# Two transformer blocks on one core: strips spread, low activations last in two tiles, feed-forward remainders on VectorE, no filler products

## The chip, the core and the metric

The kernel runs on one NeuronCore of one Trainium2 chip. The core has TensorE (PE), VectorE (DVE), ScalarE (ACT), GpSimd (POOL) and a queue for transfers (SP). The number that counts is the device time of one execution in microseconds, lower being better; the profiled execution has a time of its own beside it.

## What is computed

The reference runs 256 tokens of width 1024 through two models one behind the other, all in fp32. Each part of it has this shape (the reference, cut):

```python
h = modulate(x, norm_g[l, 0], sh1, sc1)      # rmsnorm(x) * (1 + scale) + shift
y = mixer(h)                                 # gla, or sliding window attention (swa)
x = x + g1[:, None, :] * y
h = modulate(x, norm_g[l, 1], sh2, sc2)
y = peer(h, ...)                             # product-key retrieval, u and v tables
x = x + g2[:, None, :] * y
```

The second model has the mixers mLSTM (`ml`) and latent attention (`mla`), each with a norm behind its output product, and a feed-forward part (`relu(h @ w1)` squared, `@ w2`, inner width 4096) where the first has `peer`. The vectors sh, sc and g come from `silu(c) @ mod_w + mod_b`: each is one "strip" of 8 tiles of 128x1024.

## The kernel before

**Products in three passes.** An fp32 product is made of three products of fp32r values: weight-high by activation-high, weight-high by activation-low, weight-low by activation-high. The weights stream from memory through `ring` (two slabs of two 128x1024 tiles, issued by SP). For each tile ACT makes `split_hi` (L1443), and DVE (`less_splits_vector`, L1468) or POOL (`splits_gpsimd`, L810, and `split_lo_gpsimd`, L1456) makes the remainder `split_lo = ring - split_hi`. Both are double-buffered; `hi_made`, `lo_made` count what is made, `hi_free`, `lo_free` what PE has let go. PE reads them in L698 (mixer products), L1353/L1401/L1405 and L1788 (peer), L2452/L2476/L2480 (first feed-forward product, `ffn1`) and L2494 (second, `ffn2`).

**Output products of the mixers** (`gla_out`, `swa_out`, `ml_out`, `mla_out`: `tile_gemm_M` with `last_by_tile`). PE turns the attended values (L594), ACT makes their high part (`gla_y`, `swa_y`, `ml_y`, `mla_y`, L765), DVE their low part `yT_lo` (`turned_lo_vector`, L772), and then PE takes eight weight tiles, 12 products of 128x512 each (L698). `row_store` (L486) copies a row of gains out of two banks of the accumulator memory that the product later writes. Behind the product DVE multiplies and adds the residual (L874, L885; L887 where a norm comes in between), ACT takes sums of squares (L824), DVE norms (L934, L938), and PE turns the normed tiles (L965, `tile_turn_tensor`) for the next product, the first of which are L1353 or L2452.

**Side strips.** The later modulation vectors are computed beside the mixers. POOL issues the loads (L426, `small<-in_mod`) into four slots; load n waits until DVE has used chunk n-4. DVE adds each chunk to the strip (L437 for its first chunk, L440 for the others, `side_chunks_vector`), at the places of DVE's program where the code calls it; when a strip is full PE sums it over partitions (L359, 32 products of one column), and DVE stores it (L456).

**Fillers.** `keep_busy_tensor` (L953) issues products of `ident` with `ident` into a bank that nobody reads, in nine places, 120 in all: ahead of seven turns L965, and at `swa.q` and `mla.qa` ahead of turns L579:

```python
KEEP_BUSY = {"n2_0": 8, "n1_1": 16, "n2_1": 9, "m1": 32, "m2_0": 12, "m1_1": 7, "m2_1": 9,
             "swa.q": 11, "mla.qa": 16}
```

The trace has two records for each.

**Feed-forward.** `ffn1` has 32 weight tiles of 24 products of 128x256, `ffn2` 32 tiles of 12 products of 128x512. ACT drains each pair of tiles of `ffn1` into one of four buffers (L2562, L2578); DVE squares it (L2622), rounds it to `hid_hi` (L2624) and takes `hid_lo` (L2626). POOL makes the remainders of tiles 2 to 31 of `ffn1` of both layers, tiles 0 to 3 of `ffn2` in layer 0 and all 32 in layer 1; DVE makes the other 28 of layer 0 (L1468), with the strip chunks of stage `f2_0` in between.

## Time and profile before

| | |
|---|---|
| time of three executions | 2770.6, 2771.14 and 2772.21 us (median 2771.14) |
| the profiled execution's own time | 2766.39 us |
| its span, from the first instruction to the last | 2764.8 us |
| PE busy | 2624.3 us (95%) |
| DVE busy | 2089.8 us (76%) |
| ACT busy | 1145.6 us (41%) |
| POOL busy | 714.3 us (26%) |
| data moved | 536.93 MB, 194 GB/s |

The span is what the trace's positions refer to: 1186.00 is a place 1186 us behind its start. The profiled execution took 1.6 us more than its span, and the median of the unprofiled ones lies 4.8 us above it. Busy time of PE counts matmuls, at whatever clock was granted.

### The profile page before, as it was taken

To read this page: it belongs to the slowest core of one execution; us is meant where nothing else is said; L and a number is where in the kernel's file an instruction comes from. 1 tells how busy PE (TensorE), PEld (TensorE's weight loads), DVE (VectorE), ACT (ScalarE), POOL (GpSimd) and SP (SyncE) were. 2 spreads that over 40 slices of the span, in tenths; PEclk is the share of its full clock that TensorE was granted. 3 is DMA by queue.
4 is the path that set the end of the run, shared out by engine and by line. 5 is a ranking of instruction groups with operands and counts; after the bars stand their busy time and mean duration, and the time that the engine had idled before them with its cause. 6 is when DMAs were issued, how large, how long until landed. Compare 5 with 4: busy or idle time off the path is not lost.

```text
span 2764.8 us, 51194 instructions
## 1 busy us (share of the span) xinstructions
PE 2624.3 (95%) x18482; PEld 2311.9 (84%) x18482; DVE 2089.8 (76%) x3398; ACT 1145.6 (41%) x1662; POOL 714.3 (26%) x461
## 2 busy tenths in 40 slices
PE   5989999999999999899999999999999899987998
PEld 4469999999877887789999998778888798866986
DVE  7545997777899778767987778997777798646890
ACT  1235444434434445434443334434445453322443
POOL 2001994000000000006980000000001085010787
PEclk9989999999999999999999999999999999998999
DMA  9634555444466876254555444667876446762454
GB/s 350 223 101 151 175 183 176 160 162 162 168 215 231 283 254 237 103 183 157 180 176 167 160 159 168 201 223 256 284 260 252 144 160 234 245 243 107 147 179 147
DMA packets 147627, 536.93 MB, mean 194 GB/s; under 512 B 16784, under 2 KB 17168, under 8 KB 147232
## 3 DMA queue, kind: packets, MB, share of 16 engines
q1 hardware_dynamic: 115088, 417.08, 44.7%
q0 software_dynamic: 31104, 113.26, 11.6%
q10 hardware_dynamic: 1296, 4.72, 0.4%
q8 instruction: 89, 1.46, 0.2%
q14 instruction: 50, 0.41, 0.0%
HBM read 531.85 MB, written 3.15 MB: 194 GB/s over the span
## 4 chain that ended last, share of the span: by engine, by line
PE 75%; DVE 11%; issue 6%; POOL 4%; DMA 2%; ACT 2%; DVEq 1%; SPq 0%; POOLq 0%; ACTq 0%
PE ps L1788 19%; PE ps L1401 15%; PE ps L1405 8%; PE ps L698 6%; PE ps L2494 5%; PE ps L1353 4%; POOL split_lo L1456 4%; PE ps L657 3%; PE ps L2476 3%; PE ps L1746 3%; PE ps L359 2%; DVE split_lo L1468 1%; PE ps L2480 1%; PE ps L635 1%; DMA ring<-in_stream 1%
## 5 line engine op out<-in xcount | busy, mean ns | idle before, releaser
L1443 ACT ACTIVATE split_hi<-ring 128x1024 fp32r<-128x1024 f32 x740 | 779.8, 1055 | 789.1 <-PE ps L1405 444.5
L1468 DVE TENSOR_TENSOR split_lo<-ring,split_hi 128x1024 fp32r<-128x1024 f32 x516 | 629.3, 1220 | 221.4 <-ACT split_hi L1443 221.1
L1456 POOL TENSOR_TENSOR split_lo<-ring,split_hi 128x1024 fp32r<-128x1024 f32 x208 | 551.5, 2669 | 172.1 <-ACT split_hi L1443 171.1
L376 POOL DMA_DIRECT2D mod_w<-in_mod x96 | 51.0, 531 | 1145.8 <-ACT gate L1498 426.5
L1401 PE MATMUL ps<-hT_hi,split_hi 128*128 128x256 f32 x2048 | 292.4, 285 | 0.0
L1405 PE MATMUL ps<-hT_hi,split_lo 128*128 128x256 f32 x2048 | 288.6, 284 | 2.5 <-POOL split_lo L1456 2.4
L1440 ACT ACTIVATE gate_hi<-gate 128x256 fp32r x256 | 106.9, 417 | 440.0 <-PE ps L1788 439.8
L1401 PE MATMUL ps<-hT_lo,split_hi 128*128 128x256 f32 x2048 | 287.4, 283 | 0.0
L1788 PE MATMUL ps<-split_hi,gate_hi 128*128 128x512 f32 x1024 | 284.1, 398 | 0.0
L1788 PE MATMUL ps<-split_hi,gate_lo 128*128 128x512 f32 x1024 | 276.3, 390 | 1.0 <-DVE gate_lo L1466 1.0
L1788 PE MATMUL ps<-split_lo,gate_hi 128*128 128x512 f32 x1024 | 276.6, 391 | 0.0
L1405 PEld LDWEIGHTS ps<-hT_hi,split_lo 128*128 128x128 f32 x2048 | 263.8, 192 | 5.4 <-POOL split_lo L1456 5.4
L1401 PEld LDWEIGHTS ps<-hT_lo,split_hi 128*128 128x128 f32 x2048 | 264.1, 192 | 0.0
L1401 PEld LDWEIGHTS ps<-hT_hi,split_hi 128*128 128x128 f32 x2048 | 263.0, 191 | 0.0
L1788 PEld LDWEIGHTS ps<-split_hi,gate_lo 128*128 128x128 f32 x1024 | 191.6, 188 | 43.8 <-DVE gate_lo L1466 3.0
L1788 PEld LDWEIGHTS ps<-split_lo,gate_hi 128*128 128x128 f32 x1024 | 191.4, 188 | 43.8 <-DVE split_lo L1468 3.3
L1788 PEld LDWEIGHTS ps<-split_hi,gate_hi 128*128 128x128 f32 x1024 | 187.0, 188 | 36.5 <-issue 1.4
L1466 DVE TENSOR_TENSOR gate_lo<-gate,gate_hi 128x256 fp32r<-128x256 f32 x256 | 108.0, 422 | 127.7 <-ACT split_hi L1443 127.4
L426 POOL DMA_DIRECT2D small<-in_mod x80 | 42.6, 533 | 458.1 <-DVE gate L440 319.0
L1665 DVE TENSOR_TENSOR small<-small 128x512 bf16<-128x512 bf16 x384 | 139.2, 417 | 0.0
L1746 PEld LDWEIGHTS ps<-small 128*128 128x128 bf16 x3072 | 96.8, 98 | 36.5 <-DVE small L1665 24.8
L1746 PE MATMUL ps<-small 128*128 128x64 bf16 x3072 | 111.8, 193 | 13.0 <-DVE small L1665 13.0
(383 smaller groups left out, 3886.0 us busy)
## 6 DMA issues: line engine op xcount, KB each, us to landing
ring<-in_stream SPq DMA_DIRECT2D x782, 512.0 KB, 4.1
mod_w<-in_mod POOLq DMA_DIRECT2D x96, 512.0 KB, 4.7
small<-in_mod POOLq DMA_DIRECT2D x80, 512.0 KB, 6.0
gate<-in_mod POOLq DMA_DIRECT2D x32, 512.0 KB, 9.2
gate<-in_mod ACTq DMA_DIRECT2D x8, 512.0 KB, 11.3
gate<-in_mod SPq DMA_DIRECT2D x8, 512.0 KB, 10.1
x_kept<-x POOLq DMA_DIRECT2D x4, 512.0 KB, 2.9
gate<-x_kept POOLq DMA_DIRECT2D x4, 512.0 KB, 9.1
```

The lines of the kernel that those rows point to most:

```text
L698: return nc.tensor.matmul(ps[:, banks[2 * nb + i], :], src[:, b * per + n, i * P:(i + 1) * P], w[:, b % 2, at_:at_ + BANK], start=(b == n ...
L1353: ins = nc.tensor.matmul(out, w[:, b % 2, c * P:(c + 1) * P], src[:, c, :], start=(c == 0 and w is split_hi and src is hi), stop=(c == DC ...
L1401: nc.tensor.matmul(out, split_hi[:, e, c * P:(c + 1) * P], part[:, c, :], start=(part is hT_hi and c == 0), stop=False)
L1405: ins = nc.tensor.matmul(out, split_lo[:, e, c * P:(c + 1) * P], hT_hi[:, c, :], start=False, stop=(c == DC - 1))
L1443: nc.scalar.activation(split_hi[:, e, :], ring[:, slot, e * D:(e + 1) * D], ACT.Copy).then_inc(hi_made, 1)
L1456: nc.gpsimd.tensor_tensor(split_lo[:, e, :], ring[:, slot, e * D:(e + 1) * D], split_hi[:, e, :].bitcast(F32), ALU.subtract).then_inc(lo_m ...
L1466: nc.vector.tensor_tensor(gate_lo[:, e, :], at(gate, i, 16 * SEQ, (2 * j + e) * SEQ, SEQ), gate_hi[:, e, :].bitcast(F32), ALU.subtract).th ...
L1468: nc.vector.tensor_tensor(split_lo[:, e, :], ring[:, (START[name] + j) % RING, e * D:(e + 1) * D], split_hi[:, e, :].bitcast(F32), ALU.sub ...
L1665: ins = nc.vector.tensor_tensor(pairs(hot_r[r][m]), equal, of_token(2 + m, HALF), ALU.mult)
L1746: ins = nc.tensor.matmul(ps[:, 5 + r % 2, n * HALF:(n + 1) * HALF], hot_c[r % 2][:, n, :], hot_r[r % 2][m][:, n, :], start=(m == 0), stop= ...
L1788: return nc.tensor.matmul(ps[:, 2 * nb + n, :], g[:, e, n * P:(n + 1) * P], w[:, e, nb * BANK:(nb + 1) * BANK], start=False, stop=True, sk ...
L2494: return nc.tensor.matmul(ps[:, 4 + 2 * nb + n, :], h[:, c0, n * P:(n + 1) * P], w[:, e, nb * BANK:(nb + 1) * BANK], start=(first and h is ...
```

## The change

It has seven parts. (a) In the four output products the first two weight tiles are taken by kind: weight-high and weight-low by activation-high for both tiles, and then weight-high by activation-low for both. (b) `row_store` stands ahead of `turned_lo_vector` in all four mixers. (c) The product `swa_q` writes banks 6 and 7 in place of 0 and 1. (d) All fillers are gone. (e) The strip chunks of `swa` and `mla` stand earlier in DVE's program, and none stands with the last two remainders of the output product; chunk 18 of `ml` stands earlier. (f) In `ml` the gates and the gated norms of both token tiles stand behind both attended tiles. (g) All remainders of the feed-forward parts are DVE's, between its squares; POOL issues loads only.

```diff
+            if last_by_tile:
+                for kind in (((split_hi, hi), (split_lo, hi)), ((split_hi, lo),)):
+                    for b in range(2):
+                        for w, src in kind:
+                            ready(b, w, src)
+                            for nb in range(nbs):
+                                for i in range(NT):
+                                    ins = product(b, w, src, 0, nb, i)
+                            if w is split_lo:
+                                ins.then_inc(lo_free, 1)
+                            elif src is lo:
+                                ins.then_inc(hi_free, 1)
...
+            row_store(v, "g1_0", 0)
             turned_lo_vector(v, "gla.on", yT_lo, gla_y, bank=4)
-            row_store(v, "g1_0", 0)
...
-        Q_BANKS = (2, 3, 0, 1)
+        Q_BANKS = (2, 3, 6, 7)
...
+            row_store(v, "g1_1", 4)
             turned_lo_vector(v, "swa_o", yT_lo, swa_y)
-            row_store(v, "g1_1", 4)
-            for n in range(6, 16):
-                if n < 12:
-                    less_splits_vector(v, "swa_out", n - 4, n - 3)
-                side_chunks_vector(v, "swa", n, n + 1)
+            side_chunks_vector(v, "swa", 10, 12)
+            for n in range(12, 18):
+                less_splits_vector(v, "swa_out", n - 10, n - 9)
+                if n < 16:
+                    side_chunks_vector(v, "swa", n, n + 1)
...
-            attended_vector(v, mls, ml_h, 0, [lambda: side_chunks_vector(v, "ml", 18, 19), lambda: head_gains(0)])
+            attended_vector(v, mls, ml_h, 0, [lambda: None, lambda: None])
             probT_vector(v, mls, 1)
-            heads_var_vector(v, "ml.r2", 0)
             shares(1)
-            heads_gated_vector(v, "ml.r2", 0, ml_h, ml_o, "ml.gated")
-            attended_vector(v, mls, ml_h, 1, [lambda: less_splits_vector(v, "ml_out", 0, 1), lambda: head_gains(1)])
-            heads_var_vector(v, "ml.r2", 1)
-            heads_gated_vector(v, "ml.r2", 1, ml_h, ml_o, "ml.gated")
+            attended_vector(v, mls, ml_h, 1, [lambda: head_gains(0), lambda: head_gains(1)])
+            for i in range(NT):
+                heads_var_vector(v, "ml.r2", i)
+                heads_gated_vector(v, "ml.r2", i, ml_h, ml_o, "ml.gated")
+            less_splits_vector(v, "ml_out", 0, 1)
...
+            def less(i, j, e):
+                tile = TILE0[f"ffn1_{l}"] + 2 * j + e
+                v.eng.wait_ge(hi_made, i * 8 + (tile + 1))
+                v.eng.wait_ge(lo_free, i * 8 + (tile + 1))
+                nc.vector.tensor_tensor(split_lo[:, e, :], ring[:, (START[f"ffn1_{l}"] + j) % RING, e * D:(e + 1) * D],
+                                        split_hi[:, e, :].bitcast(F32), ALU.subtract).then_inc(lo_made, 1)
+            for j in range(1, 4):
+                less(0, j, 0)
+                less(0, j, 1)
+                squares(0, j - 1)
...
+            side_chunks_vector(v, "mla", 18, 20)
+            for n in range(20, 26):
+                less_splits_vector(v, "mla_out", n - 18, n - 17)
+                if n < 24:
+                    side_chunks_vector(v, "mla", n, n + 1)
+            v.wait_ge(vector_steps, v.n)
+            tile_post_vector(v, "mla_out", "m2_1", 0)
...
             for l in range(2):
-                if l:
-                    side_loads_gpsimd(g, "mla")
-                splits_gpsimd(g, f"ffn1_{l}", 2, 8)
-                split_lo_gpsimd(g, f"ffn1_{l}", 1, 4)
-                if l:
-                    split_lo_gpsimd(g, "ffn2_1", 0, 4)
-                else:
-                    splits_gpsimd(g, "ffn2_0", 0, FFN2_FIRST)
-                    side_loads_gpsimd(g, "f2_0")
+                side_loads_gpsimd(g, ("f2_0", "mla")[l])
```

`squares(i, j)` holds the three instructions of L2622 to L2626. The functions' lines move: L486 keeps its number, L772 becomes L784, L1468 becomes L1459, L874 becomes L876, L2622 to L2626 become L2616 to L2620, and the loop's remainders are L2626.

PE's program at the start of `gla_out`, as a difference (- before, + changed), where `gla_y` is the high part of the activations and `yT_lo` the low part:

```order
 L594 MATMUL ps<-ident,gate 128x128 x16
 L698 MATMUL ps<-split_hi,gla_y 128x512 x4
-L698 MATMUL ps<-split_hi,yT_lo 128x512 x4
 L698 MATMUL ps<-split_lo,gla_y 128x512 x4
 L698 MATMUL ps<-split_hi,gla_y 128x512 x4
-L698 MATMUL ps<-split_hi,yT_lo 128x512 x4
 L698 MATMUL ps<-split_lo,gla_y 128x512 x4
+L698 MATMUL ps<-split_hi,yT_lo 128x512 x8
 L698 MATMUL ps<-split_hi,gla_y 128x512 x4
```

The two groups of products with `yT_lo` have moved from behind 4 and 16 products to behind 16, as one group of 8. It is the same in the other three output products.

DVE's program at the end of `mla_out`, before (from the last but two remainder on; L1468 is a remainder, L440 a strip chunk, L874 the first step behind the product):

```order
L1468 TENSOR_TENSOR split_lo<-ring,split_hi 128x1024
L440 SCALAR_TENSOR_TENSOR gate<-small,c_act,gate 128x1024
L1468 TENSOR_TENSOR split_lo<-ring,split_hi 128x1024
L440 SCALAR_TENSOR_TENSOR gate<-small,c_act,gate 128x1024
L1468 TENSOR_TENSOR split_lo<-ring,split_hi 128x1024
L440 SCALAR_TENSOR_TENSOR gate<-small,c_act,gate 128x1024 x4
L486 COPY gate<-ps 128x512 x2
L874 TENSOR_TENSOR gate<-ps,gate 128x512 x2
```

And the same place in the changed kernel (L1459 is the remainder, L876 the first step behind the product):

```order
L1459 TENSOR_TENSOR split_lo<-ring,split_hi 128x1024
L440 SCALAR_TENSOR_TENSOR gate<-small,c_act,gate 128x1024
L1459 TENSOR_TENSOR split_lo<-ring,split_hi 128x1024
L440 SCALAR_TENSOR_TENSOR gate<-small,c_act,gate 128x1024
L1459 TENSOR_TENSOR split_lo<-ring,split_hi 128x1024 x2
L876 TENSOR_TENSOR gate<-ps,gate 128x512 x2
L857 TENSOR_SCALAR stat<-stat 128x1
```

The four chunks at the end and the copy of the gain row L486 have moved ahead of the product, and two remainders stand together at the end.

DVE's program at the start of the loop of `ffn1_0`, before (`gate` is the drained buffer; ISA and REGISTER_ALU rows carry waits and addresses):

```order
L2622 TENSOR_TENSOR gate<-gate 128x512
L2623 ISA
L2624 ISA
L2624 COPY hid_hi<-gate 128x512
L2625 REGISTER_ALU
L2626 REGISTER_ALU
L2626 TENSOR_TENSOR hid_lo<-gate,hid_hi 128x512
```

And its first rows in the changed kernel, where L2626 is now the remainder and L2616 the square:

```order
L2626 TENSOR_TENSOR split_lo<-ring,split_hi 128x1024 x2
L2616 TENSOR_TENSOR gate<-gate 128x512
L2618 CAST hid_hi<-gate 128x512
L2620 TENSOR_TENSOR hid_lo<-gate,hid_hi 128x512
L2626 TENSOR_TENSOR split_lo<-ring,split_hi 128x1024 x2
```

Two remainders now stand ahead of each square. POOL's program over the same stretch and up to the start of layer 1, before (it makes the remainders of L810 and L1456 and issues the strip loads L426):

```order
L810 TENSOR_TENSOR split_lo<-ring,split_hi 128x1024 x4
L426 DMA small<-in_mod 128x1024 x40
L810 TENSOR_TENSOR split_lo<-ring,split_hi 128x1024 x6
L1449 UNCONDITIONAL_BRANCH
L1449 ISA
L1456 TENSOR_TENSOR split_lo<-ring,split_hi 128x1024
```

And the end of POOL's program in the changed kernel:

```order
L376 DMA mod_w<-in_mod 128x1024
L383 REGISTER_ALU
L383 COMPARE_AND_BRANCH
L2867 DMA gate<-x_kept 128x1024 x2
L426 DMA small<-in_mod 128x1024 x64
L131 UNCONDITIONAL_BRANCH
```

The 64 loads of both layers now stand in one row behind each other, each held only by its slot; no remainder is left on POOL.

## Rows read from the trace of the kernel before

**Rows 1.** The page: busy time, costliest groups (busy, mean ns), DMA issues (to landing).

```profile
PE 2624.3 (95%) x18482; PEld 2311.9 (84%) x18482; DVE 2089.8 (76%) x3398; ACT 1145.6 (41%) x1662; POOL 714.3 (26%) x461
...
L1456 POOL TENSOR_TENSOR split_lo<-ring,split_hi 128x1024 fp32r<-128x1024 f32 x208 | 551.5, 2669 | 172.1 <-ACT split_hi L1443 171.1
...
small<-in_mod POOLq DMA_DIRECT2D x80, 512.0 KB, 6.0
```

**Rows 2.** Waits of PE (engine, line, releaser: us in total, times, longest).

```profile
PE ps L359 <- DVE gate L874: 10.9, 2, 5.9
```

**Rows 3.** Timeline, start of `gla_out` (start, us, instruction, xcount, [idle before, releaser]).

```profile
174.60 2.48 DVE L772 TENSOR_TENSOR yT_lo<-ps,gla_y 128x512 fp32r<-128x512 f32 x4 [1.16 <-ACT gla_y L765]
177.00 1.28 DVE L486 COPY gate<-ps 128x512 f32<-128x512 f32 x2
...
178.38 2.04 PE L698 MATMUL ps<-split_hi,gla_y 128*128 128x512 f32 x4 [3.79 <-DVE gate L486]
```

**Rows 4.** Windows, the same place (stretch, length, busy per engine, granted clock PEclk).

```profile
176.00:183.00 7.00, 4.62 (x12) 3.66 (x13) 2.27 (x4) 0.38 (x2) 0.00 (x0) 0.52 0.00 0
```

**Rows 5.** Timeline, start of `swa_q`.

```profile
1090.25 1.69 PE L698 MATMUL ps<-split_hi,own_hi 128*128 128x512 f32 x4 [2.00 <-ACT gate L1871]
1091.20 0.87 DVE L789 SCALAR_TENSOR_TENSOR hT<-ps,scale_c,own_hi 128x256 f32<-128x256 f32 x2
```

**Rows 6.** Timeline, from the last product of `swa_out` to the next product.

```profile
1186.00 0.40 PE L698 MATMUL ps<-split_lo,swa_y 128*128 128x512 f32 x1
...
1189.33 1.29 DVE L440 SCALAR_TENSOR_TENSOR gate<-small,c_act,gate 128x1024 f32<-128x1024 f32 x1 [1.22 <-DMA small<-in_mod]
...
1191.40 6.99 PE L359 MATMUL ps<-ones,gate 128*128 128x1 f32 x32 [5.00 <-DVE gate L874]
...
1198.25 4.19 PE L953 MATMUL ps<-ident 128*128 128x128 f32 x18
...
1204.85 3.49 PE L1353 MATMUL ps<-hT_hi,split_hi 128*128 128x256 f32 x8 [0.17 <-ACT hT_hi L981]
```

**Rows 7.** Timeline, behind the last product of `gla_out`.

```profile
202.60 1.95 PE L953 MATMUL ps<-ident 128*128 128x128 f32 x16
...
209.55 3.48 PE L1353 MATMUL ps<-hT_hi,split_hi 128*128 128x256 f32 x8 [0.86 <-ACT hT_hi L981]
```

**Rows 8.** Timeline, start of `ml_out`.

```profile
2182.66 2.05 PE L698 MATMUL ps<-split_hi,ml_y 128*128 128x512 f32 x4 [2.95 <-DVE yT_lo L772]
```

**Rows 9.** Timeline, end of `mla_out`.

```profile
2548.12 0.40 PE L698 MATMUL ps<-split_lo,mla_y 128*128 128x512 f32 x1
2551.18 1.28 DVE L440 SCALAR_TENSOR_TENSOR gate<-small,c_act,gate 128x1024 f32<-128x1024 f32 x1 [2.58 <-DMA small<-in_mod]
```

**Rows 10.** Timeline of PE, first product behind `mla_out`.

```profile
2567.32 0.36 PE L2452 MATMUL ps<-mlp_hi,split_hi 128*128 128x256 f32 x1 [0.15 <-ACT mlp_hi L981]
```

**Rows 11.** Timeline, end of `ml_out` (L359 stands right behind its last product).

```profile
2206.81 3.69 PE L359 MATMUL ps<-ones,gate 128*128 128x1 f32 x32
...
2217.11 0.35 PE L2452 MATMUL ps<-mlp_hi,split_hi 128*128 128x256 f32 x1 [0.51 <-ACT mlp_hi L981]
```

**Rows 12.** Timeline, from `ffn1_0` to `ffn2_0`.

```profile
2320.08 2.92 DVE L2622 TENSOR_TENSOR gate<-gate 128x512 f32<-128x512 f32 x1
...
2324.30 0.68 DVE L2622 TENSOR_TENSOR gate<-gate 128x512 f32<-128x512 f32 x1
...
2329.54 1.95 PE L2494 MATMUL ps<-split_lo,hid_hi 128*128 128x512 f32 x4 [3.80 <-DVE split_lo L1468]
2330.07 1.22 DVE L1468 TENSOR_TENSOR split_lo<-ring,split_hi 128x1024 fp32r<-128x1024 f32 x1
```

**Rows 13.** Windows, `ffn1_0` with its first `ffn2` tiles, and `ffn2_1`.

```profile
2245.00:2329.00 84.00, 79.58 (x614) 75.86 (x612) 80.44 (x42) 35.45 (x40) 73.28 (x31) 1.00 0.57 189
...
2662.00:2753.00 91.00, 89.68 (x379) 70.98 (x380) 31.75 (x15) 33.91 (x35) 81.12 (x32) 1.00 0.51 165
```

**Rows 14.** Timeline, the 32 fillers of `m1`.

```profile
2062.52 7.31 PE L953 MATMUL ps<-ident 128*128 128x128 f32 x64
```

More of the change, by code:

```diff
@@ L713, in ready @@
                     t.wait_ge(*when((lo_mark if src is lo else hi_mark)(b * per + n)))
-            for b in range(tiles - (2 if last_by_tile else 0)):
+            if last_by_tile:
[10 more added lines that the diff above has]
+                                ins.then_inc(hi_free, 1)
+            for b in range(2 if last_by_tile else 0, tiles - (2 if last_by_tile else 0)):
                 for w, src in kinds:
@@ L801, in less_splits_vector @@
                 split_lo_vector(v, name, 0, b // 2, b % 2)
-        def splits_gpsimd(g, name, first, last):
-            g.eng.wait_ge(lo_made, TILE0[name] + first)
-            for b in range(first, last):
-                tile = TILE0[name] + b
-                g.eng.wait_ge(hi_made, tile + 1)
-                g.eng.wait_ge(lo_free, tile + 1)
-                nc.gpsimd.tensor_tensor(split_lo[:, b % 2, :], ring[:, (START[name] + b // 2) % RING, (b % 2) * D:(b % 2 + 1) * D],
-                                        split_hi[:, b % 2, :].bitcast(F32), ALU.subtract).then_inc(lo_made, 1)
         def half(nb):
@@ L943, in scale_vector @@
                                            op0=ALU.add, op1=ALU.mult).then_inc(vector_steps, v.step(f"{name}.scale"))
-        KEEP_BUSY = {"n2_0": 8, "n1_1": 16, "n2_1": 9, "m1": 32, "m2_0": 12, "m1_1": 7, "m2_1": 9,
-                     "swa.q": 11, "mla.qa": 16}
-        def keep_busy_tensor(t, place, bank):
-            for mark in free[bank]:
-                t.wait_ge(*when(mark))
-            for _ in range(KEEP_BUSY[place]):
-                nc.tensor.matmul(ps[:, bank, 0:P], ident[:, :], ident[:, :], start=True, stop=True)
         def tile_turn_tensor(t, name, bank, read_by):
-            keep_busy_tensor(t, name, bank)
             for i in range(NT):
@@ L2127, in swa_vector @@
                 less_splits_vector(v, "swa_q", b, b + 1)
+            side_chunks_vector(v, "swa", 0, 2)
             for i in range(NT):
@@ L2421, in mlstm_vector @@
                     side_chunks_vector(v, "ml", n, n + 1)
-            post_rest_vector(v, "ml_out", 4, 0, "m2_0")
+            v.wait_ge(vector_steps, v.n)
+            tile_post_vector(v, "ml_out", "m2_0", 0)
         MLP = Area(gate, LAYER)
@@ L2428, in build, with ffn2_less_vector @@
         MLP_STEPS = FF // P // 8
-        FFN2_FIRST = 4
-        def ffn2_less_vector(v):
-            v.eng.wait_ge(lo_made, TILE0["ffn2_0"] + FFN2_FIRST)
-            for b in range(FFN2_FIRST, FF // P):
-                less_splits_vector(v, "ffn2_0", b, b + 1)
-                n = b - FFN2_FIRST
-                if n % 4 < 3 and n - n // 4 < DC * len(SIDE_STRIPS["f2_0"]):
+        def ffn2_less_vector(v, l, first, last):
+            for b in range(first, last):
+                less_splits_vector(v, f"ffn2_{l}", b, b + 1)
+                n = b - 4
+                if l == 0 and n >= 0 and n % 4 < 3 and n - n // 4 < DC * len(SIDE_STRIPS["f2_0"]):
                     side_chunks_vector(v, "f2_0", n - n // 4, n - n // 4 + 1)
@@ L2627, in mlp_vector @@
+            with v.eng.Fori(1, MLP_STEPS) as i:
+                for j in range(4):
+                    less(i, j, 0)
+                    less(i, j, 1)
+                    if j:
+                        squares(i, j - 1)
+                    else:
+                        squares(i - 1, 3)
             v.seen.clear()
-            if l == 0:
-                ffn2_less_vector(v)
+            ffn2_less_vector(v, l, 0, 2)
+            squares(MLP_STEPS - 1, 3)
+            ffn2_less_vector(v, l, 2, FF // P)
@@ L2730, in mla_vector @@
                     .then_inc(vector_steps, v.step())
-            side_chunks_vector(v, "mla", 10, 14)
+            side_chunks_vector(v, "mla", 6, 12)
             for i in range(NT):
```

43 lines of the change are left out of this document (21 added, 22 removed).

## The prediction

> **What bounds the kernel now.** I read the page first. PE is busy for 2624.3 of 2764.8 us [rows 1], so PE's program sets the time, and a change can only give what lies in the remaining 140 us, or in stretches in which PE runs at the lower of its two clocks. POOL makes 208 remainders at a mean of 2.67 us each, and a strip load takes 6.0 us from issue to landing [rows 1]. Second, the waits of PE, to see which engine ends them. The largest that the change touches is that of the strip sums L359 on DVE, 10.9 us in two places [rows 2]. Third, the timeline around each of these waits, where the reader is to see what DVE did just before it let PE go. Fourth, the granted clock of the same stretches: behind the wait of 3.79 us ahead of `gla_out` it is 0.52 over 7 us [rows 4], that is 1.2 GHz. So a wait of PE costs twice: itself, and the slower products behind it.
>
> Unit prices. In `ffn2_1` 379 records of products of 128x512 filled 89.68 us [rows 13], 0.237 us each; a weight tile of 12 such products is 2.8 us, and so is one of `ffn1`, 24 products of half the width. A pair of tiles is 5.7 us. A filler record at full clock takes 7.31 / 64 = 0.114 us [rows 14].
>
> **Gains.** *Start of `gla_out`.* DVE made `yT_lo` from 174.60 on, then copied the gain row (two copies, from 177.00, 1.28 us together), and only then could PE begin, at 178.38 [rows 3]. DVE had been idle for 1.16 us ahead of 174.60 [rows 3], so the row copy, moved in front, ends near 174.8, and PE begins there: 3.6 us earlier. `yT_lo` then ends at 174.8 + 2.5 = 177.3, and its first product stands 16 products later, not before 174.8 + 16 x 0.237 = 178.6. Some of the half clock goes with the wait; the first four products took 2.04 us [rows 3] for 4 x 0.237 = 0.95. I take 1 us. Sum **4.5**, between 3.6 and 5.9 (3.6 and the 4.6 us behind 178.38 in [rows 4] at full clock, 2.3).
>
> *The other three starts.* There the turned values stand in the banks that the product writes, so PE still waits until DVE has read them for `yT_lo`; parts (a) and (b) bring nothing. In `ml` part (f) lets DVE come to `yT_lo` earlier, since the step ahead of it loses a chunk (1.29 us [rows 6]). PE began at 2182.66 after 2.95 us of waiting for it [rows 8]; I take **1.5**, between 0 and 2.95.
>
> *End of `swa_out`.* The last product starts at 1186.00, so the gemm ends near 1186.2. DVE is still adding chunks until 1189.33 + 1.29, partly waiting for the loads; PE's L359 starts at 1191.40 after 5.00 us idle, its 32 products take 6.99 us at half clock, the 9 fillers 4.19 (0.233 per record, twice 0.114), and the next product starts at 1204.85 [rows 6, 14]. That is 18.6 us. Behind `gla_out`, the same code without chunks, it is 209.55 - 202.60 = 6.95 us [rows 7]. With the chunks ahead, `swa_out` should look like that; I take 0.5 us off for the strip's sum and store: **11.2**, between 5.0 (the wait alone) and 11.7.
>
> *End of `mla_out`.* 2548.35 to 2567.32, 19.0 us [rows 9, 10], with DVE held by a chunk whose load landed 2.58 us late [rows 9]. Behind `ml_out`, whose chunks end in time, it is 2206.81 to 2217.11, 10.3 us [rows 11]. Difference 8.7, and 0.5 as in the next item: **9.2**, between 5.9 (the wait in [rows 2]) and 9.5.
>
> *Fillers that held PE.* At `m2_0` and `m1_1` fillers ran at half clock and ended behind the normed tile. By 0.233 per record, 12 and 7 of them are up to 5.6 and 3.3 us long; I estimate **1.5** for both, 0 to 3.
>
> *Feed-forward, layer 0.* While POOL makes remainders, a square takes 2.92 us, and 0.68 once it has stopped [rows 12]. DVE is therefore late: it comes to the `ffn2` remainder after its last squares, PE waits 3.80 us for it, and the next four products take 1.95 us, half clock [rows 12]. In the window PE lacks 84.0 - 79.6 = 4.4 us [rows 13]. With remainders on DVE, a pair costs it 2 x 1.22 + 3 x 0.68 = 4.5 us [rows 12] of the 5.7 that PE takes, if no POOL instruction competes. I count 4.4, and 1.7 for two groups of four products at half clock: **6.1**, between 3.8 and 8. *Layer 1* had no such wait; 91.0 - 89.7 = **1.3** [rows 13], 0 to 3.
>
> A page speaks to this step. The Trainium skill, "SBUF — State Buffer", section "Who interferes with whom", says that a VectorE instruction with two SBUF inputs and a GpSimd instruction that reads SBUF exclude each other for their whole length. The square has both inputs in SBUF, and 2.92 against 0.68 us agrees [rows 12]. By the same section the strip loads, which GpSimd issues, can be held by VectorE copies and casts; no run here shows by how much, and that rule stands beside rival C.
>
> Gains: 4.5 + 1.5 + 11.2 + 9.2 + 1.5 + 6.1 + 1.3 = **35.3 us**.
>
> **Losses.** *Fillers that covered a real wait.* At `n2_0`, `n1_1`, `swa.q`, `m1` and `mla.qa` the fillers (8, 16, 11, 32, 16) ran for 1.9, 3.7, 2.5, 7.3 and 3.7 us at 0.114 per record [rows 7, 14] while PE had to wait for the norm or the rotation anyway. Without them PE is idle for that long and a little more. The nearest row is `gla_out`: 3.79 us of idling, then half clock over 7 us [rows 3, 4], 4.6 of them with products, which costs 2.3 us; with work throughout it would be 3.5. Below, 0: another wait of the same length, 2.95 us ahead of `ml_out`, was already paid. Much of the half clock can also fall on turns that wait for ACT. I take 1.0, 1.7, 1.2, 1.2 and 1.7: **6.8**, between 0 and 17.5. At `n2_1` and `m2_1` there was no full clock to lose.
>
> *`swa_q` in banks 6 and 7.* These banks hold the turned values that DVE reads in its last L789, at 1091.20 + 0.87 = 1092.07; PE began at 1090.25 [rows 5]. PE now waits 1.85 us more, with about 1 us of clock behind it: **2.9**, between 0 (if the first banks give it enough) and 4.
>
> *High parts late.* `hi_free` for the first tile comes after 20 products, not after 9. 20 x 0.237 + 1.1 for ACT is 5.8 us, and the third tile is due at 24 x 0.237 = 5.7; with the two signals 0.4 us late: **1.6** over four products, 0 to 3.
>
> *Chunks ahead of the rotations.* They are 1.29 us each [rows 6] in places where DVE mostly waits; **0.8** in all, 0 to 4. What is queued behind them is the rotation, and PE's turns wait for it.
>
> Losses 6.8 + 2.9 + 1.6 + 0.8 = **12.1 us**. The row copies, the move of the gates in `ml` and POOL's loads cost nothing, since DVE was idle or POOL, with nothing but loads left in its queue, had only its slots to wait for; if the cover were gone, a row copy would cost 1.28.
>
> **Sum.** -35.3 + 12.1 = -23.2. The profiled execution would go from 2766.4 to 2743, the median from 2771.1 to **2748 us** (0.8%).
>
> **Rivals.** *A, the sum as above*: 0.66, 2738 to 2756.
> *B, the clock takes more.* PE falls back to 1.2 GHz at each of the five covered waits for 7 us, 3.5 each, 17.5 in place of 6.8: -12.5, 2759. For it: [rows 4]. Against: part of that time PE waits in any case. 0.15. The Trainium skill, "TensorE: Matmul & The Clock Gate", section "HAM oscillation — how this bites in real kernels", says that idle gaps of PE put it back to the low clock and that the work behind pays; by it this case would be B.
> *C, strips still late.* Loads take 6.0 us with four slots, so a chunk can come every 1.5 us, and DVE's queue has remainders of the output product behind each. If a load is late the remainder is late, and PE waits inside the gemm in place of its end. Half of 20.4 is given back: -13, 2758. For it: DVE waits for loads in both ends [rows 6, 9]. Against: the chunks start earlier by several tiles. 0.08.
> *D, slower: DVE becomes the bound of the feed-forward.* The remainder waits behind the square in DVE's order, and the square behind ACT's drain. If a pair takes DVE 7.0 us in place of 4.5, 32 pairs lose 1.3 each, 42 us, and the 7.4 gained are gone: +26, 2797. It outweighs the rest from about 6.4 us per pair. Against: 1.2 us of room per pair. 0.04.
> *E, the feed-forward change does nothing*, because the squares stay at 2.9 us for another reason or the seam wait stays: -16, 2755. 0.07.
>
> **Range and chances.** A, C and E lie at 2738 to 2758 and B around 2759, so 2737 to 2761 leaves out D and the tails of A and B. A measurement of this kernel tells about 0.2% (5.5 us) from no change. Faster: A, C, E nearly whole and most of B, 0.91; same, mostly from B with more losses, 0.05; slower, D, 0.04.
>
> **What would show it.** Squares of about 0.7 us throughout; no wait on DVE at the start of `ffn2_0`; no POOL remainder; `gla_out` at about 175; L359 right behind the last product of `swa_out` and `mla_out`, and 7 and 10 us to the next product; `swa_q` waiting for DVE L801; half-clock stretches where the five fillers were. The prediction is wrong if L359 still waits, if PE waits for L2626 in the feed-forward, or if half-clock stretches of 7 us follow at more than two of the five places where fillers covered a wait.

## The result, and the profile after

The changed kernel takes 2749.27 us (median of 4 executions, 2745.64 to 2754.17) where the kernel before takes 2771.68: ratio 0.9915, interval 0.9892 to 0.9938. Measured again beside the last experiments it took 2749.86 us (6 executions) against 2772.42, ratio 0.9923 (0.9906 to 0.994). It is 0.8% faster. The forecast was 2748 us, in 2737 to 2761.

The profiled execution took 2747.67 us, 18.7 less than that of before; the forecast for it was 2743. The page of the changed kernel, its span, busy times and the two groups of remainders (busy us, mean ns, idle before and releaser):

```profile
span 2746.0 us, 50625 instructions
...
PE 2599.7 (95%) x18242; PEld 2288.9 (83%) x18242; DVE 2049.4 (75%) x3494; ACT 1144.9 (42%) x1662; POOL 459.1 (17%) x365
...
L1459 DVE TENSOR_TENSOR split_lo<-ring,split_hi 128x1024 fp32r<-128x1024 f32 x552 | 673.1, 1220 | 273.4 <-ACT split_hi L1434 273.1
L1447 POOL TENSOR_TENSOR split_lo<-ring,split_hi 128x1024 fp32r<-128x1024 f32 x128 | 341.1, 2681 | 148.9 <-ACT split_hi L1434 148.6
```

PE is busy for 24.6 us less than before [rows 1], with 240 records fewer, which are the fillers'; so PE's busy time says nothing of the gain. POOL makes 128 remainders where it made 208 [rows 1]. DVE makes the others, in this group and in the new line L2626.

The waits of PE that the change touched (engine, line, releaser: us in total, times, longest):

```profile
PE ps L956 <- DVE stat L857: 18.7, 5, 8.0
...
PE ps L698 <- DVE yT_lo L784: 11.0, 3, 5.3
PE ps L657 <- DMA ring<-in_stream: 8.5, 2, 5.1
...
PE ps L579 <- DVE gate L2733: 4.5, 1, 4.5
PE ps L698 <- DVE hT_lo L807: 4.2, 1, 4.2
```

L359 on L874, first in [rows 2], no longer stands there. In its place stand waits that fillers had covered (L956 is the turn of a normed tile, L579 on L2733 the one at `mla.qa`), and the new one of `swa_q` on L807.

The two ends of output products, in the timeline of the changed kernel, `swa_out` first. The rows are the strip's sum, the turns and the next product:

```profile
1189.68 3.84 PE L359 MATMUL ps<-ones,gate 128*128 128x1 f32 x32
...
1193.38 3.38 PE L956 MATMUL ps<-ident,gate 128*128 128x128 f32 x16
...
1196.62 3.66 PE L1344 MATMUL ps<-hT_hi,split_hi 128*128 128x256 f32 x8
```

```profile
2541.89 4.33 PE L359 MATMUL ps<-ones,gate 128*128 128x1 f32 x32
...
2548.19 3.53 PE L956 MATMUL ps<-ident,gate 128*128 128x128 f32 x16 [1.97 <-DVE stat L857]
...
2552.18 0.35 PE L2446 MATMUL ps<-mlp_hi,split_hi 128*128 128x256 f32 x1 [0.46 <-ACT mlp_hi L972]
```

L359 stands right behind the product now, at full clock (3.84 us for 32, 6.99 in [rows 6]). From the last product of `swa_out` (1189.44) to the next product it is 7.2 us where it was 18.9, and behind `mla_out` (2541.66) 10.5 where it was 19.2 [rows 6, 9, 10]. Both are what the ends of `gla_out` and `ml_out` show [rows 7, 11].

DVE in `ffn1_0` of the changed kernel, groups by line (busy us, mean ns, idle before, releaser). L2626 is the remainder, L2616 the square, L2618 the high part, L2620 the low part:

```profile
L2626 DVE TENSOR_TENSOR split_lo<-ring,split_hi 128x1024 fp32r<-128x1024 f32 x22 | 26.9, 1223 | 14.2 <-ACT split_hi L1434 14.2
L2620 DVE TENSOR_TENSOR hid_lo<-gate,hid_hi 128x512 f32 x12 | 8.3, 693 | 1.5
L2616 DVE TENSOR_TENSOR gate<-gate 128x512 f32<-128x512 f32 x11 | 7.5, 684 | 0.0
L2618 DVE CAST hid_hi<-gate 128x512 f32 x11 | 4.7, 427 | 1.6 <-DVE gate L2616 0.3
```

Every square takes 0.68 us, where [rows 12] has 2.92. Windows over the two feed-forward products of layer 0 (length, busy of PE, PEld, DVE, ACT, POOL, granted clock, DMA share, GB/s):

```profile
2241.00:2305.00 64.00, 64.00 (x546) 64.00 (x545) 46.74 (x57) 28.97 (x34) 0.00 (x0) 1.00 0.58 188
2307.00:2400.00 93.00, 93.00 (x411) 74.78 (x409) 62.12 (x63) 34.47 (x39) 8.45 (x16) 1.00 0.78 269
```

PE has no idle time in either, at full clock, where it lacked 4.4 us before [rows 13]; DVE is busy for 46.7 of 64 us.

The stages compare as follows. Each number is the distance between the starts of two instructions of PE's program in a trace: first to last product of an output product, the last product of one to the first of the next, and so on (us). `peer` and `ffn2_0` end with their last weight-high by activation-high product, and `mLSTM` begins with its first product. The last column is the predicted difference. Where the prediction has one number for two places, it is shared out here: the chunks ahead of the rotations by halves, the 1.5 of the fillers that held PE by their number (12 and 7).

| stage | before | changed | changed, second profile | predicted |
|---|---|---|---|---|
| start of the last eight turns L594 to first product of `gla_out` | 4.9 | 1.3 | 1.3 | -3.6 |
| `gla_out` | 24.0 | 22.6 | 22.6 | -0.6 |
| `peer`, layer 0 | 857.8 | 859.7 | 863.1 | 0 |
| key and value product to start of `swa_q` | 15.5 | 17.6 | 17.7 | +1.9 |
| `swa_q` | 23.7 | 24.3 | 24.3 | +1.0 |
| swa attention | 49.8 | 53.1 | 50.3 | +1.6 |
| `swa_out` | 22.2 | 22.8 | 22.8 | +0.4 |
| to the next product | 18.9 | 7.2 | 7.8 | -11.2 |
| `peer`, layer 1 | 857.0 | 860.9 | 859.4 | 0 |
| mLSTM up to `ml_out` | 109.2 | 107.2 | 105.5 | -1.5 |
| `ml_out` | 23.9 | 25.5 | 24.9 | +0.4 |
| `ffn1_0` and `ffn2_0` | 191.6 | 183.6 | 183.6 | -6.1 |
| from there to `mla_out` | 117.2 | 122.5 | 124.7 | +1.5 |
| `mla_out` | 22.2 | 22.8 | 22.8 | +0.4 |
| to the next product | 19.2 | 10.5 | 10.5 | -9.2 |
| `ffn1_1` and `ffn2_1` | 187.7 | 184.1 | 184.1 | -1.3 |

The profiled execution of before was itself on the low side: 30 more executions of that kernel ran from 2763.24 to 2777.08 with a median of 2771.14. One kernel's executions spread over 0.5%, so for an edit of a few us the stages of the traces say more than the times, and only where they repeat.

### The profile page after: what moved, and what is told of

The parts are those of the page before. It is cut to its first block, busy times and chain, and to the rows that moved or that the text cites. A ratio compares the mean times of both kernels' runs of the same rounds, so it can differ in the third digit from the quotient of the medians.

```text
span 2746.0 us, 50625 instructions
## 1 busy us (share of the span) xinstructions
PE 2599.7 (95%) x18242; PEld 2288.9 (83%) x18242; DVE 2049.4 (75%) x3494; ACT 1144.9 (42%) x1662; POOL 459.1 (17%) x365
## 4 chain that ended last, share of the span: by engine, by line
PE 78%; DVE 10%; issue 4%; POOL 3%; DMA 2%; ACT 2%; DVEq 0%; SPq 0%; POOLq 0%; ACTq 0%
PE ps L1779 20%; PE ps L1392 15%; PE ps L1396 8%; PE ps L2488 6%; PE ps L698 5%; PE ps L2470 4%; PE ps L1344 4%; POOL split_lo L1447 3%; PE ps L657 3%; PE ps L1737 3%; PE ps L2474 2%; DVE split_lo L1459 2%; PE ps L635 1%; DMA ring<-in_stream 1%; PE ps L359 1%
## 5 line engine op out<-in xcount | busy, mean ns | idle before, releaser
L1459 DVE TENSOR_TENSOR split_lo<-ring,split_hi 128x1024 fp32r<-128x1024 f32 x552 | 673.1, 1220 | 273.4 <-ACT split_hi L1434 273.1
L1447 POOL TENSOR_TENSOR split_lo<-ring,split_hi 128x1024 fp32r<-128x1024 f32 x128 | 341.1, 2681 | 148.9 <-ACT split_hi L1434 148.6
L426 POOL DMA_DIRECT2D small<-in_mod x80 | 42.2, 528 | 561.9 <-DVE gate L440 315.3
## 6 DMA issues: line engine op xcount, KB each, us to landing
gate<-in_mod SPq DMA_DIRECT2D x8, 512.0 KB, 10.2
```

The source lines that it names most:

```text
L1447: nc.gpsimd.tensor_tensor(split_lo[:, e, :], ring[:, slot, e * D:(e + 1) * D], split_hi[:, e, :].bitcast(F32), ALU.subtract).then_inc(lo_m ...
L1459: nc.vector.tensor_tensor(split_lo[:, e, :], ring[:, (START[name] + j) % RING, e * D:(e + 1) * D], split_hi[:, e, :].bitcast(F32), ALU.sub ...
```

## The experiments

Eleven kernels, and the changed one again, in three groups; each group has its own executions of the kernel before beside it. Ratios are to those, with 95% intervals.

### The feed-forward change alone

```diff
 # kernel before, with part (g) only
-            with v.eng.Fori(0, MLP_STEPS) as i:
+            for j in range(1, 4):
+                less(0, j, 0)
+                less(0, j, 1)
+                squares(0, j - 1)
+            with v.eng.Fori(1, MLP_STEPS) as i:
...
-                splits_gpsimd(g, f"ffn1_{l}", 2, 8)
-                split_lo_gpsimd(g, f"ffn1_{l}", 1, 4)
```

> The kernel before with part (g) alone: all feed-forward remainders on VectorE, POOL only issues loads. Theory (the sum): the seam wait of 3.80 us at ffn2_0, the half clock behind it and the small waits of POOL's remainders go; profiled span 7 to 12 us below before (11.7 is what the positions of the two traces differ by over both layers), nothing else moves. Rival E (the squares stay at 2.9 us or the seam wait stays): within 3 us of before. Rival D (VectorE the bound): slower by over 10 us.

2759.45 us, ratio 0.9971 (0.9957 to 0.9984), 4 to 12 us faster. In its trace the four products, those of `ffn1` up to the start of `ffn2`, are 93.4, 90.6, 93.8 and 91.1 us long, 10.5 less in sum than before, and a square takes 0.68 us. Rivals D and E fall: neither did DVE become the bound, nor did the squares stay slow. About a third of what the whole change gives is there without any other part.

### The strips alone

```diff
 # kernel before, with the chunks of swa and mla as in the change
+            side_chunks_vector(v, "mla", 18, 20)
+            for n in range(20, 26):
+                less_splits_vector(v, "mla_out", n - 18, n - 17)
+                if n < 24:
+                    side_chunks_vector(v, "mla", n, n + 1)
             post_rest_vector(v, "mla_out", 4, 0, "m2_1")
```

> The kernel before with the chunks of swa and mla spread as in the change, and nothing else (fillers, row copies, banks as before). Theory: the ends of swa_out and mla_out shrink by about 11 and 9 us, less 2 to 5 us that the chunks ahead of the rotations and the strip loads beside the ring loads cost inside the two attentions: 15 to 19 us faster. Rival (the strips merely move their cost): under 8 us faster, with the remainders of the output products late.

2757.83 us, ratio 0.9956 (0.994 to 0.9973), 7 to 17 us faster. The two ends went to 9.5 and 11.2 us, 17.4 less together; the attention of swa is 0.7 us longer, `mla_out` 1.3 with 3 us at half clock in it, and `ffn1_1` with `ffn2_1` behind it 1.4. Rival C falls: L359 waits in neither place, and little of the cost has moved. The profiled span fell by only 8.6, with `peer` 2.8 us longer in each layer, where nothing was edited; what that is comes below.

Both parts together are 0.9927 by these ratios, and the whole change is 0.9915 and 0.9923. So the other five parts together bring nothing that these measurements can tell.

### No fillers, nothing else

```diff
-        KEEP_BUSY = {"n2_0": 8, "n1_1": 16, "n2_1": 9, "m1": 32, "m2_0": 12, "m1_1": 7, "m2_1": 9,
-                     "swa.q": 11, "mla.qa": 16}
+        KEEP_BUSY = {}
```

> The kernel before without the 120 fillers, and nothing else. Theory: the four fillers in stretches that ran at half clock anyway (n2_1, m2_0, m1_1, m2_1) give 4 to 8 us back, the five that covered a wait cost 5 to 8 us: within 4 us of before. Rival B (the clock falls at each of the five and takes 3.5 us): slower by 8 to 14 us. Second rival (the fillers did nothing): faster by 5 to 8 us.

2772.62 us, ratio 0.9997 (0.9985 to 1.001): no difference. By stages it is give and take: 3.4 us less at `n2_1` and 1.2 at `m2_1`, 2.7 more in the swa attention, 3.3 more up to `mla_out`, 0.7 at `n1_1`. The prediction's signs hold (some places gain, others lose), and both rivals fall: the fillers did something, and their absence did not cost 8 us or more.

### The order of products, and the row copy, in two steps

```diff
 # e4: kernel before, with
+                for kind in (((split_hi, hi), (split_lo, hi)), ((split_hi, lo),)):
 # e4 and e12: kernel before, with
+            row_store(v, "g1_0", 0)
             turned_lo_vector(v, "gla.on", yT_lo, gla_y, bank=4)
-            row_store(v, "g1_0", 0)
```

With both, for the first tiles of all four output products:

> The kernel before with low activations last in the first two tiles of the four output products, and the gain row copied ahead of the low part in gla alone. Theory: gla_out starts 3.8 us earlier and its end is 5 us earlier; each of the four products loses 0.4 us at its third tile; 3 to 4 us faster in all at equal clock elsewhere. Rival (the clock of later stages moves as much): the gain at the end of gla_out is there, but the sum over the span differs from it by over 3 us.

2776.25 us, ratio 1.0019 (1.0008 to 1.0029): slower, where 3 to 4 us faster were expected. The start of `gla_out` improved as predicted (1.25 us from the start of the last eight turns, 4.9 before).

With the row copy alone:

> The kernel before with nothing but the gain row copied ahead of the low part in gla (no change of the order of products). Theory: from the last turn L594 to the first product falls from 4.9 to 1.25 us, gla_out falls to 22.0 since the low part arrives in four pieces in time, the other output products stay at 22.2 and 23.9: 4 to 6 us faster than before at equal clock, ratio 0.998. Rival (the gain is paid back by the clock of later stages, as in the run with the new order, 0.19% slower): ratio 1.000 to 1.002.

2773.31 us, ratio 1.0002 (0.9991 to 1.0012). From the last eight turns to the first product it is 1.25 us here too, and `gla_out` 22.05 where it is 22.55 with the new order. So the row copy gives all of the gain at this place, and the order takes some back: by the traces of these two kernels 0.5 us in each of `gla_out`, `swa_out` and `mla_out` and 1.6 in `ml_out`, 3.2 in sum. In the trace with the new order the end of `swa_out` was also 2.3 us longer (21.2 and 18.9). Its profiled execution was the fastest of its twelve, so the trace need not show all of what made the median slower. The expected 4 to 6 us faster did not come for the row copy; its `peer` stages were 863.1 and 864.6 us, 5 and 8 longer than in the profile of before, and the last section takes them apart.

### The changed kernel with the old order of products

```diff
-            if last_by_tile:
-                for kind in (((split_hi, hi), (split_lo, hi)), ((split_hi, lo),)):
...
-            for b in range(2 if last_by_tile else 0, tiles - (2 if last_by_tile else 0)):
+            for b in range(tiles - (2 if last_by_tile else 0)):
```

> The changed kernel with the old order of products (high, low, then the weight's low part) in the first two tiles of the four output products; the row copies stay ahead. Theory: swa_out and mla_out fall from 22.8 to 22.2 us, ml_out from 25.5 to about 23.9, and the start of gla_out comes 1 to 2.5 us later, since yT_lo is needed after 4 products: together within 2 us of the changed kernel. Rival (the order itself costs, as the run with it alone, 0.19% slower than before, suggests): 4 to 6 us faster than the changed kernel.

2747.83 us, ratio 0.9914 (0.9889 to 0.9939), no different from the changed kernel; the rival, 4 to 6 us faster, did not come. `gla_out` and `mla_out` fell to 22.0 and 22.2 us, while `swa_out` took 23.8 where 22.2 was expected: PE ran its first tile at 1.2 GHz, four products in 1.91 us. `ml_out` was 24.9, as in the second profile of the changed kernel. The trace shows why the order is not needed. The start of `gla_out` (start, us, instruction, xcount):

```profile
174.97 2.48 DVE L772 TENSOR_TENSOR yT_lo<-ps,gla_y 128x512 fp32r<-128x512 f32 x4
...
175.11 1.17 PE L698 MATMUL ps<-split_hi,gla_y 128*128 128x512 f32 x4 [0.15 <-DVE gate L486]
...
176.12 1.09 PE L698 MATMUL ps<-split_hi,yT_lo 128*128 128x512 f32 x4
...
177.05 1.08 PE L698 MATMUL ps<-split_lo,gla_y 128*128 128x512 f32 x4
```

DVE makes `yT_lo` from 174.97 to 177.45, and PE takes its first product with it at 176.12, without a wait: in the code DVE signals each of the four copies by itself, and the first tile needs only the first. The same rows of the changed kernel:

```profile
173.23 1.28 DVE L486 COPY gate<-ps 128x512 f32<-128x512 f32 x2
...
173.37 1.09 PE L594 MATMUL ps<-ident,gate 128*128 128x128 f32 x8 [1.09 <-DVE gate L541]
...
174.48 2.48 DVE L784 TENSOR_TENSOR yT_lo<-ps,gla_y 128x512 fp32r<-128x512 f32 x4
...
174.62 1.16 PE L698 MATMUL ps<-split_hi,gla_y 128*128 128x512 f32 x4 [0.15 <-DVE gate L486]
...
178.37 2.02 PE L698 MATMUL ps<-split_hi,yT_lo 128*128 128x512 f32 x8
```

PE begins at 174.62, 1.25 us behind the start of its last eight turns at 173.37, as in the other kernel. The row copy L486 now fills DVE's idle time ahead of `yT_lo`.

### The fillers put back

```diff
 # e5: all nine places; e6: the five places that cover a wait
+        KEEP_BUSY = {"n2_0": 8, "n1_1": 16, "m1": 32, "swa.q": 11, "mla.qa": 16}
```

> The changed kernel with all 120 fillers put back in their nine places. What is known: taking them out of the kernel before changed its time by -0.03% (interval -0.15 to +0.10). Theory: the same here, the five that cover a wait give 6 to 9 us back, the four others take 4 to 8 us: within 4 us of the changed kernel, ratio to before 0.990 to 0.993. Rival (with the chunk waits gone, the fillers of n2_1 and m2_1 run at full clock and are cheap): 5 us faster than the changed kernel.

All of them: 2746.03 us, ratio 0.9903 (0.9881 to 0.9926), not to be told from the changed kernel. Behind `swa_out` its stage is 9.5 us in place of 7.2, behind `mla_out` 11.2 in place of 10.5: there the fillers are in the way. This is one trace; what repeats is that the two ends of e2, which has the same fillers, are 9.5 and 11.2 us too.

> The changed kernel with fillers only in the five places where PE waits anyway: n2_0 8, n1_1 16, m1 32, swa.q 11, mla.qa 16. Theory: the clock of n1_1, the swa attention and the mla attention comes back (0.7, about 2, about 3.3 us by the stages of the run without fillers), and of the peer stages behind them where it had fallen: 5 to 12 us faster than the changed kernel, ratio to before 0.987 to 0.990. Rival (clock falls come by chance and even out): no different from the changed kernel.

The five: 2741.81 us, ratio 0.9895 (0.9872 to 0.9918), 7.5 us under the changed kernel in the median, but the two intervals overlap. The stage up to `mla_out` is 117.7 us, 4.8 less than in the changed kernel, the swa attention 50.0; `mla_out` itself is 1.3 us longer, with 2.9 us at half clock. Here is PE at `mla.qa` in the changed kernel, the last key product, and the turns behind the wait:

```profile
2427.67 4.74 PE L657 MATMUL ps<-ring,gate 128*128 128x320 f32 x17
2436.91 2.40 PE L579 MATMUL ps<-ident,gate 128*128 128x128 f32 x10 [4.51 <-DVE gate L2733]
```

and in the kernel with the fillers of `swa.q` and `mla.qa` alone (below), the fillers and the turns:

```profile
2427.98 3.73 PE L942 MATMUL ps<-ident 128*128 128x128 f32 x32
2432.65 1.31 PE L579 MATMUL ps<-ident,gate 128*128 128x128 f32 x10 [0.94 <-DVE gate L2733]
```

The same 10 turns take 2.40 us behind 4.51 us of idling and 1.31 behind the fillers. Over all fourteen profiles the stage took 120.4 to 124.7 us in the five without this filler (mean 122.5) and 116.0 to 120.0 in the nine with it (mean 117.9). This is the one place where a filler is worth something every time, 4.6 us in the mean, and not all of that is clock: without it PE then waits 4.4 to 6.3 us for a ring load (L657), with it 2.2 to 3.5. It does so with the old places of the strips too, so their new places are not the cause; why the load comes later was not settled.

### `swa_q` in its old banks

```diff
-        Q_BANKS = (2, 3, 6, 7)
+        Q_BANKS = (2, 3, 0, 1)
```

> The changed kernel with swa_q in banks 2, 3, 0, 1 again. Theory: PE no longer waits for the last L801 (stage kv 17.64 back to 15.5 us), and the half clock behind it shortens: 2 to 4 us in the profile, ratio to before 0.988 to 0.991. Rival (the banks only move the wait, since the first tiles need the same values): stage kv falls by under 0.5 us.

2746.1 us, ratio 0.9902 (0.988 to 0.9923). The stage ahead of `swa_q` is 15.5 us again, 2.2 less than in the changed kernel, whose trace shows the wait:

```profile
1088.00 0.87 DVE L801 SCALAR_TENSOR_TENSOR hT<-ps,scale_c,own_hi 128x256 f32<-128x256 f32 x2
1088.79 0.60 DVE L807 TENSOR_SCALAR hT_lo<-hT,modc 128x256 fp32r<-128x256 f32 x2
...
1089.23 2.05 PE L698 MATMUL ps<-split_hi,own_hi 128*128 128x512 f32 x4 [4.17 <-DVE hT_lo L807]
```

The last L801, which reads the banks, and the last L807 run to the start of PE's first product; PE idles for 4.17 us, 2.00 in [rows 5]. The rival, that the banks only move the wait, falls by the length of the stage; the whole time is too coarse to show 2 us.

### Two versions put together

```diff
 # changed kernel, old banks, old order of products, and
+        KEEP_BUSY = {"n2_0": 8, "n1_1": 16, "m1": 32, "swa.q": 11, "mla.qa": 16}   # e9
+        KEEP_BUSY = {"swa.q": 11, "mla.qa": 16}                                    # e10
```

> The changed kernel itself once more, beside the next three on the same chip, since executions of one kernel spread over 10 to 17 us. Expected: 2741 to 2755 us, ratio to before 0.989 to 0.993, stages as in its first profile but for peer0, peer1 and the start, which differed by up to 5 us between profiles of the same code.

> The changed kernel with the five fillers that cover a wait (n2_0, n1_1, m1, swa.q, mla.qa), swa_q in banks 2, 3, 0, 1, and the old order of products in the first two tiles. Theory: stage sums add up, 8.5 us of clock in the two attentions and ml, 2.2 at the start of swa_q, about 1.5 in the output products: 9 to 13 us faster than the changed kernel, ratio to before 0.985 to 0.988. Rival (the clock of peer and of the start decides and is chance): within 4 us of the run with the five fillers alone.

> As the run before, with the fillers of swa.q and mla.qa alone. Theory: the two attentions are where the clock came back (3.1 and 4.8 us); n2_0, n1_1 and m1 showed under 0.6 us in their own stages. So within 3 us of the run with five. Rival (fillers at norms also keep the clock of the stage behind them): 4 to 8 us slower than the run with five, lost in kv, m1 and ml.

The changed kernel again took 2749.86 us, ratio 0.9923 (0.9906 to 0.994). With five fillers it was 2745.53, 0.99 (0.9874 to 0.9927), 4 us less than the changed kernel where 9 to 13 were expected; by its own words the rival holds, within 4 us of the kernel with the five fillers alone (2741.81). With the two it was 2738.03, 0.9878 (0.9856 to 0.99), and this one lies clear of the changed kernel measured beside it: the two intervals do not meet. It was expected within 3 us of the version with five and lies 7.5 under it, with intervals that overlap. So the fillers at the three norms are not missed. Between the two versions the stages with edits differ by under 1 us each but for `swa_q` (22.1 and 23.7); the stage that differs most in the two profiles is `peer` of layer 1, 864.3 and 857.5, in which no edit lies.

## Why the prediction was right, point by point

**The two ends of the output products** were predicted at 11.2 and 9.2 us and came to 11.7 and 8.7. Reading the neighbour of the same code without chunks at its end ([rows 7, 11]) gave the size of the new stage, not only of the wait, and that held within 0.5 us.

**The feed-forward** was right in mechanism (DVE's squares slowed by POOL, a late DVE at the seam) and too small: 8.0 us in layer 0 where 6.1 were predicted, and 3.7 in layer 1 where 1.3 were. The terms that were too small counted only what the window calls idle [rows 13], and in layer 1 they looked at `ffn2_1` alone, while half of the gain, 1.9 us, came in `ffn1_1` and the step from it to `ffn2_1`. Other gaps, small ones between products, are covered by the busy time and only show in the length of the stage: `ffn2_1` went from 92.9 to 91.1 us though its idle time had been 1.3. In time, the part alone gave 4 to 12 us. Rival D's working has a slip: the change would come out even at 6.2 us per pair (the other terms' 15.8 us over 32 pairs, and 5.7), not 6.4.

**The start of `gla_out`**: 3.6 us for the wait, as predicted, and 1.4 net in `gla_out`, where 0.6 was taken. Wrong is the step "its first product stands 16 products later" as the reason that PE need not wait. With the old order it does not wait either, so part (a) has no gain anywhere, and costs 0.5 us for each product, 0.4 predicted, by the late high parts (PE waits 0.28 us for ACT's `split_hi` at the third tile of `gla_out`, at 180.67 in the changed kernel). For `ml_out` the pairs of traces with and without the order give 0 to 1.6 us.

**The fillers** were predicted at 6.8 us of loss, spread over five places. The places are wrong: `n2_0`, `n1_1` and `m1` lose 0.1, 0.1 to 0.7 and 0.4 us where 1.0, 1.7 and 1.2 were taken, and `mla.qa` loses 4.6 where 1.7 was. In the swa attention two profiles of the same changed kernel give 53.1 and 50.3 us, so there it is partly chance. At `m2_0` and `m1_1`, where 1.5 us of gain was taken, removing them gave little: `m2_0` is 10.5 us in every profile, with and without, and at `m1_1` the first product comes 0.8 us sooner than in before. The step that failed is to price the clock by one wait of like length: the length of the idle time does not say what follows.

One of the prediction's own signs of being wrong was met in the first profile: half-clock stretches of about 7 us at more than two of the five places. Windows inside them, for `n2_0`, `n1_1`, `swa.q`, `m1` and `mla.qa` (length, busy of PE, PEld, DVE, ACT, POOL, granted clock, DMA share, GB/s):

```profile
199.80:206.40 6.60, 5.26 (x21) 4.73 (x21) 5.01 (x14) 5.05 (x12) 0.53 (x1) 0.50 0.47 172
1070.20:1073.40 3.20, 3.20 (x11) 2.45 (x10) 2.81 (x6) 2.97 (x6) 0.00 (x0) 0.50 0.95 356
1117.90:1128.00 10.10, 7.41 (x43) 7.01 (x44) 6.03 (x18) 0.38 (x1) 0.00 (x0) 0.50 0.25 100
2063.40:2070.10 6.70, 3.78 (x18) 3.74 (x18) 4.70 (x12) 5.57 (x13) 0.00 (x0) 0.50 0.52 210
2435.50:2442.10 6.60, 5.19 (x18) 4.56 (x19) 5.17 (x23) 0.00 (x0) 0.00 (x0) 0.50 0.24 95
```

The stretches themselves are 6.8, 3.4, 10.2, 6.8 and 6.8 us long. Four of the five reach that length, so by this sign the prediction would be wrong; in the second profile they are 6.8, 3.4, 3.4, 6.8 and 3.4, and two do. The sign says less than the prediction took it to say: at `n2_0` the clock is halved for 6.8 us, of which PE is busy for about 5, and the stage is only 0.1 us longer.

**`swa_q` in other banks** cost 2.2 us at its start, and up to 0.6 in it, 2.9 predicted. The 2.2 repeat in all three kernels with the old banks. The 0.6 do not: three other kernels with the new banks have `swa_q` at 23.5 to 23.7 us, as before.

**`ml`** gave 2.0 and 3.7 us in the two profiles, 1.5 predicted. Part (f) was not run by itself, so that this gain is its doing is argued from the stage alone. The **chunks ahead of the rotations**, 0.8 predicted, made the swa attention 0.7 us longer in the kernel with the strips alone and the stage up to `mla_out` 1.2 us shorter, so no loss is shown.

**What no term had** is `peer`. The parts of the kernel that are not edited were longer by 1.8 and 3.9 us in the first profile of the changed kernel and 5.3 and 2.4 in the second. The terms that were too small and this cancel, so it is partly luck that 2748 us came closer than the single steps did. Rival B named the clock as what could take more, and it did, at `mla.qa` and in `peer`, which is not one of its five places; the rest of what `peer` took is waits for loads, as the last section shows.

## What to carry to other kernels

Price a stage that loses a wait by a stage of the same code that has no such wait, since the clock and the tail come with it. Look at whether a producer signals in pieces before reordering its consumer. Where executions of one kernel spread by more than the edit is worth, compare the lengths of stages over several traces and trust those that repeat; a filler product is worth keeping only where that shows, here in one of nine places.

## What the runs showed of the hardware

The clock granted to the same instructions differs between profiles. In `peer` of layer 0, PE takes 24 small products, 16 products of one column (L359) and goes on with wide ones. In the changed kernel:

```profile
811.51 0.87 PE L1737 MATMUL ps<-small 128*128 128x64 bf16 x24 [0.30 <-DVE small L1656]
812.22 1.93 PE L359 MATMUL ps<-ones,mod_acc 128*128 128x1 f32 x16
814.00 2.01 PE L1779 MATMUL ps<-split_hi,gate_hi 128*128 128x512 f32 x4
815.82 1.85 PE L1779 MATMUL ps<-split_hi,gate_lo 128*128 128x512 f32 x4
817.50 1.08 PE L1779 MATMUL ps<-split_lo,gate_hi 128*128 128x512 f32 x4
```

and the same instructions in the kernel before, 6 us later in the span:

```profile
817.44 0.87 PE L1746 MATMUL ps<-small 128*128 128x64 bf16 x24 [0.23 <-DVE small L1665]
818.15 1.93 PE L359 MATMUL ps<-ones,mod_acc 128*128 128x1 f32 x16
819.94 1.18 PE L1788 MATMUL ps<-split_hi,gate_hi 128*128 128x512 f32 x4
820.95 1.07 PE L1788 MATMUL ps<-split_hi,gate_lo 128*128 128x512 f32 x4
```

Nearly the same idle time ahead, the same 1.93 us of narrow products, and then 2.01 us for four wide products in one and 1.18 in the other: 1.2 GHz in one case and 2.4 in the other, 1.6 us lost over 12 products. Each `peer` has six such groups of 16 narrow products. Over the fourteen profiles a stretch of 3.4 us at half clock stood behind the first or the second of them in many, and never right behind the other four. Behind the first group of layer 0 it stood in nine of the ten profiles in which `gla_out` starts earlier, and in none of the four in which it doesn't. In layer 1 the changed kernel had it behind both groups in one profile and behind neither in the other, so there the program alone does not decide it.

The other part of `peer` is no matter of the clock. These are rows of the kernel with the row copy alone:

```profile
902.18 1.28 DVE L396 SCALAR_TENSOR_TENSOR mod_acc<-mod_w,c_act,mod_acc 128x1024 f32<-128x1024 f32 x1 [2.25 <-DMA mod_w<-in_mod]
903.38 0.42 DVE L1466 TENSOR_TENSOR gate_lo<-gate,gate_hi 128x256 fp32r<-128x256 f32 x1
...
903.86 1.19 PE L1788 MATMUL ps<-split_hi,gate_lo 128*128 128x512 f32 x4 [1.97 <-DVE gate_lo L1466]
```

DVE waits 2.25 us for a load of modulation weights, makes `gate_lo` only behind it, and PE waits 1.97 us for that. In all fourteen traces each of the 35 waits of over 0.5 us for `gate_lo` stands behind such a load that came late. In this kernel they are 3.5 us in layer 0, where before has 1.0, and 3.9 in layer 1, where before has none. In each layer it also has 6.8 us more at half clock than before, which is 3.4 us of work lost. Together these come to 5.9 and 7.3 us, where the stages are 5.3 and 7.7 longer. In the kernel with the strips alone most of the 2.8 us of layer 0 are such waits (3.4 us where before has 1.0), with no more half clock than before; in layer 1 they are 1.0, and 1.7 are clock.

Over the fourteen profiles `peer` of layer 0 took 857.5 to 864.3 us, with 3.4 to 13.7 us of it at half clock, and it was 2.7 us longer in the mean of the ten in which `gla_out` starts earlier (861.6) than in the four in which it doesn't (858.9). That moving the start causes either part is suggested by these counts and means and was not tried by itself, and why the loads come late was not followed. The first 170 us vary too, by up to 9 us from one profile to the next of kernels that are the same until there, with 14 to 41 us of them at half clock. The Trainium skill, "TensorE: Matmul & The Clock Gate", section "HAM oscillation — how this bites in real kernels", has idle gaps as what returns PE to the low clock; the rows above do not bear that out as the whole rule, since PE had been idle for only 0.30 and 0.23 us ahead, and the clock was low in one alone.
